# Mixer A's queries turned by VectorE, ScalarE and GpSimd instead of TensorE, the rotation on VectorE alone, and the score units one pair later

## The reference, cut to what matters

```
q_raw = q.reshape(b, N_KV_A, GROUP_A, s_len, dh) * scale
q_rot = rope(q, pos).reshape(b, N_KV_A, GROUP_A, s_len, dh) * scale
...
sc = jnp.einsum('bhgtd,bhcd->bhgtc', q_raw, kc)          # compressed branch: raw queries
p_cmp = jax.nn.softmax(jnp.where(c_valid, sc, NEG), axis=-1) * c_valid.any(-1)[:, None]
...
num, _, den = band_attention(q_rot, rope(k_win, pos), v_win, WIN - 1)   # window branch: rotated queries
o = gates[..., 0:1] * o_cmp + gates[..., 1:2] * o_slc + gates[..., 2:3] * o_win
```

## Time and profile before

| what | us |
|---|---|
| median of three runs (lowest to highest) | 1766.12 (1765.85 to 1766.53) |
| the profiled execution: its own time | 1765.85 |
| its span, first to last instruction | 1763.9 |
| TensorE busy (matmuls) | 1757.8 |
| VectorE busy | 1153.4 |
| ScalarE busy | 886.8 |
| GpSimd busy | 598.9 |

### The profile page before, as it was taken

The page is one execution under the profiler, slowest core; times in us unless marked ns, Lnnn a source line. Parts: engine busy times, 40 slices in busy tenths (PEclk is TensorE's granted clock), DMA queues, the critical chain, the costliest instruction groups (busy, mean ns, idle before and its releaser), DMA issues.

```text
span 1763.9 us, 22877 instructions
## 1 busy us (share of the span) xinstructions
PE 1757.8 (100%) x7902; PEld 1456.4 (83%) x7902; DVE 1153.4 (65%) x1192; ACT 886.8 (50%) x1216; POOL 598.9 (34%) x834
## 2 busy tenths in 40 slices
PE   9999999999999999999999999999999999999998
PEld 7888888888888888888888888888888888888886
DVE  7657656787888878656665666566655784444445
ACT  7643455464554545456435643564456554444443
POOL 3335303367593948721353034304431510000000
PEclk9999999999999999999999999999999999999999
DMA  9866687656565656666666666666666656667665
GB/s 294 254 199 188 188 248 229 179 161 185 157 189 151 185 160 174 183 197 182 179 195 196 182 181 197 194 190 176 191 194 191 190 185 217 213 213 212 213 202 204
DMA packets 184267, 344.77 MB, mean 195 GB/s; under 512 B 15216, under 2 KB 19568, under 8 KB 184176
## 3 DMA queue, kind: packets, MB, share of 16 engines
q1 hardware_dynamic: 183456, 342.58, 66.2%
q10 hardware_dynamic: 720, 0.93, 0.1%
HBM read 339.27 MB, written 4.19 MB: 195 GB/s over the span
## 4 chain that ended last, share of the span: by engine, by line
PE 99%; DMA 0%; ACT 0%; SPq 0%; DVE 0%; ACTq 0%; issue 0%
PE acc L640 31%; PE acc L646 31%; PE acc L643 31%; PE acc L821 1%; PE scores L810 0%; PE scores L709 0%; DMA raw<-in_w_in 0%; PE scores L742 0%; PE scores L741 0%; PE scores L740 0%; PE heads L757 0%; PE heads L758 0%; PE heads L759 0%; PE scores L665 0%; PE heads L692 0%; PE trans L657 0%
## 5 line engine op out<-in xcount | busy, mean ns | idle before, releaser
L1239 DVE TENSOR_TENSOR w_parts<-raw,w_parts 128x1024 fp32r<-128x1024 f32 x620 | 784.4, 1266 | 556.9 <-ACT w_parts L929 555.3
L929 ACT ACTIVATE w_parts<-raw 128x1024 fp32r<-128x1024 f32 x620 | 656.2, 1059 | 662.6 <-PE acc L646 649.6
L640 PE MATMUL acc<-w_parts,x_parts 128*128 128x512 f32 x2424 | 946.7, 391 | 0.2 <-DVE w_parts L1239 0.2
L646 PE MATMUL acc<-w_parts,x_parts 128*128 128x512 f32 x2424 | 943.8, 389 | 0.0
L643 PE MATMUL acc<-w_parts,x_parts 128*128 128x512 f32 x2424 | 943.3, 389 | 0.0
L646 PEld LDWEIGHTS acc<-w_parts,x_parts 128*128 128x128 f32 x2424 | 455.1, 188 | 95.8 <-DVE x_parts L1281 0.3
L640 PEld LDWEIGHTS acc<-w_parts,x_parts 128*128 128x128 f32 x2424 | 455.3, 188 | 93.4 <-issue 0.6
L643 PEld LDWEIGHTS acc<-w_parts,x_parts 128*128 128x128 f32 x2424 | 455.3, 188 | 93.0
L515 POOL COPY rot<-tok_b 32x256 f32<-32x256 f32 x120 | 86.9, 724 | 140.6 <-DVE tok_b L1613 135.7
L499 POOL TENSOR_TENSOR rot<-tok_a,trig 128x512 f32<-128x512 f32 x18 | 30.6, 1699 | 260.5 <-ACT tok_a L935 121.4
L515 POOL COPY b_first_t<-probs 32x128 f32<-32x128 f32 x64 | 31.1, 485 | 163.1 <-DVE probs L1686 160.6
(11 more groups left out here) (240 smaller groups left out, 1010.1 us busy)
## 6 DMA issues: line engine op xcount, KB each, us to landing
raw<-in_w_in SPq DMA_DIRECT2D x478, 512.0 KB, 3.7
raw<-in_w_out SPq DMA_DIRECT2D x128, 512.0 KB, 4.3
raw<-in_w SPq DMA_DIRECT2D x16, 512.0 KB, 4.7
x_tok<-in_x SPq DMA_DIRECT2D x16, 256.0 KB, 5.3
xt_raw<-in_x_t SPq DMA_DIRECT2D x7, 512.0 KB, 6.2
wpost<-in_post_w SPq DMA_DIRECT2D x8, 256.0 KB, 5.1
out<-y SPq DMA_DIRECT2D x3, 512.0 KB, 2.8
out<-y SPq DMA_DIRECT2D x5, 256.0 KB, 2.1
```

Source lines behind the costliest of these rows:

```text
L640: nc.tensor.matmul(o, stat_hi, mov_hi, start=(k == 0), stop=False)
L646: last = nc.tensor.matmul(o, stat_lo, mov_hi, start=False, stop=(k == KB - 1))
L929: nc.scalar.activation(w_hi[:, n % SPLIT_SLOTS, :, 0:width], raw[:, n % RAW_SLOTS, :, 0:width], ACT.Copy).then_inc(hi_ready, 1)
L1239: V.tensor_tensor(w_lo[:, s, :, 0:width], raw[:, n % RAW_SLOTS, :, 0:width], w_hi[:, s, :, 0:width].bitcast(F32), ALU.subtract).then_inc(l ...
```

## The change

TensorE's eight batches of four transposes go, and with them ScalarE's evacuations. VectorE transposes all of `tok_a` within its 32x32 blocks in one instruction at `at` 0; then GpSimd moves the eight blocks of the first 64 partitions and ScalarE the eight of the others (four at `at` 1, four at `at` 2) into `qraw_t`. GpSimd's part in the rotation goes: at `at` 2 VectorE multiplies both tiles by the cosines, makes the two crossed halves into `mixed`, and adds. The compressed scores move from pair 3 to pair 4, their product with the values from pair 11 to 12, the turn of their rows from `at` 5 to `at` 7. The units move from pairs 6, 7, 8, 10, 12, 14 to 7, 8, 9, 11, 13, 14. GpSimd's last two batches of moved probabilities are announced one after the other, not both at the end.

```diff
-UNIT_STEPS = {6: 0, 7: 1, 8: 2, 10: 3, 12: 4, 14: 5}
+UNIT_STEPS = {7: 0, 8: 1, 9: 2, 11: 3, 13: 4, 14: 5}
...
             def rotate_a(g):
-                for t in range(TILES):
...
-                    pool.wait_ge(tr_free, FILL_A + t + 1 + FILLS_A * g)
-                    nc.gpsimd.tensor_tensor(turned, qraw_t[:, :, cols], cos, ALU.mult).then_inc(q_cos_ready, 1)
-                    pool.wait_ge(q_cos_ready, t + 1 + 2 * g)
-                    pool.wait_ge(q_sin_ready, t + 1 + 2 * g)
-                    nc.gpsimd.tensor_tensor(turned, turned, crossed, ALU.add).then_inc(q_rot_ready, 1)
+                pool.wait_ge(q_turned, g + 1)
+                move_blocks(tok_a[:, :, :].rearrange("p t (h d) -> p t h d", h=HPG),
+                            qraw_t[:, :, :].rearrange("p h (t q) -> p t h q", t=TILES),
+                            range(QUARTERS * QUARTERS // 2)).then_inc(q_moved_pool, 1)
+                pool.wait_ge(q_moved_pool, g + 1)
                 pool.wait_ge(q_ready, 2 + 2 * g)
...
-                    last.then_inc(probs_moved, 1)
+                        if i == 1:
+                            last.then_inc(probs_moved, 1)
...
-                if n in (1, 2):
-                    t = n - 1
-                    pe.wait_ge(acc0_free if t == 0 else acc1_free, c)
-                    transpose4(tok_a[:, t, :], fill + t)
-                if n == 3:
-                    pe.wait_ge(tr_free, fill + 2)
+                if n == 4:
+                    pe.wait_ge(q_moved_pool, g + 1)
+                    pe.wait_ge(q_moved_act, g + 1)
...
-                if n == 11:
+                if n == 12:
                     pe.wait_ge(rows_moved, g + 1)
...
             def first_turned(u, g):
-                act.wait_ge(probs_moved, 3 * g + (1 if u < 2 else 3))
+                act.wait_ge(probs_moved, 3 * g + u // 2 + 1)
...
                     if at in (1, 2):
-                        take_fill(fill + at - 1, qraw_t[:, :, (at - 1) * P:at * P])
+                        if at == 1:
+                            act.wait_ge(q_turned, g + 1)
+                        for cols in range(QUARTERS):
+                            last = move_quarters(tok_a, qraw_t, at + 1, cols)
+                        if at == 2:
+                            last.then_inc(q_moved_act, 1)
...
+            def rotate_queries(g):
+                dve.wait_ge(q_moved_pool, g + 1)
+                dve.wait_ge(q_moved_act, g + 1)
...
+                V.tensor_tensor(turned, source, factor[1], ALU.mult)
                 for x in range(2):
...
+                    own, other = slice(x * 64, (x + 1) * 64), slice((1 - x) * 64, (2 - x) * 64)
+                    last = V.tensor_tensor(crossed[own, :, :, :], source[other, :, :, :], factor[0][other, :, :, :], ALU.mult)
                 last.then_inc(q_sin_ready, 1)
+                dve.wait_ge(q_sin_ready, g + 1)
+                V.tensor_tensor(turned, turned, crossed, ALU.add).then_inc(q_rot_ready, 1)
...
-                    if at in (2, 3):
-                        crossed_halves(at - 2, g, fill)
+                    if at == 0:
+                        dve.wait_ge(acc0_free, c)
+                        dve.wait_ge(acc1_free, c)
+                        V.transpose(tok_a[:, :, :], tok_a[:, :, :]).then_inc(q_turned, 1)
+                    if at == 2:
+                        rotate_queries(g)
...
+                    if at == 7:
+                        dve.wait_ge(probs_ready, unit + 1)
+                        rows = rows_c[:, :, :, :, :].rearrange("p t h a c -> p (t h a c)").bitcast(F32)
+                        V.transpose(rows, rows).then_inc(rows_turned, 1)
...
-                    if at == 5:
-                        dve.wait_ge(probs_ready, unit + 1)
-                        rows = rows_c[:, :, :, :, :].rearrange("p t h a c -> p (t h a c)").bitcast(F32)
-                        V.transpose(rows, rows).then_inc(rows_turned, 1)
```

More of the change, by code:

```diff
@@ L315, in build @@
         heads_taken = sem("heads_taken")
-        q_cos_ready = sem("q_cos_ready")
+        q_turned = sem("q_turned")
+        q_moved_pool = sem("q_moved_pool")
+        q_moved_act = sem("q_moved_act")
         q_sin_ready = sem("q_sin_ready")
@@ L651, in gemm_pair @@
                     last.then_inc(last_tile0, 1)
[L653 to L658, removed]
             def first_scores(unit, g):
@@ L727, in attention_a, with scores_a @@
                 if n in UNIT_STEPS:
-                    scores_a(UNIT_STEPS[n], g, unit, fill)
-            def scores_a(u, g, unit, fill):
+                    scores_a(UNIT_STEPS[n], g, unit)
+            def scores_a(u, g, unit):
                 t = UNIT_TILES_A[u]
@@ L864, in _, with attention_a_chunk @@
                 gemm_pair(C_QA0, n, 0)
-            def attention_a_chunk(c, g, fill, unit):
+            def attention_a_chunk(c, g, unit):
                 for n in range(PAIRS):
-                    attention_a(n, c, g, fill, unit)
+                    attention_a(n, g, unit)
                     gemm_pair(c, n, 1)
             for g in range(GROUPS - 1):
-                per = FILLS_A
-                attention_a_chunk(C_A + 2 * g, g, FILL_A + per * g, UNITS_A * g)
+                attention_a_chunk(C_A + 2 * g, g, UNITS_A * g)
                 for n in range(PAIRS):
@@ L876, in _ @@
                     gemm_pair(C_A + 1 + 2 * g, n, 0)
[L877 removed]
+            attention_a_chunk(C_B - 1, GROUPS - 1, UNIT_B - UNITS_A)
             for g in range(GROUPS):
@@ L1065, in move_quarters, with attention_a_frame @@
                                             ACT.Copy)
-            def attention_a_frame(c, g, fill, unit):
+            def attention_a_frame(c, g, unit):
                 for n in range(LEAD, PAIRS + LEAD):
@@ L1153, in _ @@
             with act.Fori(0, GROUPS - 1) as g:
-                per = FILLS_A
-                attention_a_frame(C_A + 2 * g, g, FILL_A + per * g, UNITS_A * g)
+                attention_a_frame(C_A + 2 * g, g, UNITS_A * g)
                 mixing_frame(C_A + 1 + 2 * g, 2 * g, g)
-            attention_a_frame(C_B - 1, GROUPS - 1, FILL_B - FILLS_A, UNIT_B - UNITS_A)
+            attention_a_frame(C_B - 1, GROUPS - 1, UNIT_B - UNITS_A)
             mixing_frame(C_B, 2 * (GROUPS - 1), GROUPS - 1)
@@ L1504, in rest_turned @@
                                 ).then_inc(pt_ready, 1)
[L1506 to L1510, removed]
+            def rotate_queries(g):
+                dve.wait_ge(q_moved_pool, g + 1)
+                dve.wait_ge(q_moved_act, g + 1)
+                by_tile = "p h (t q) -> p t h q"
+                turned = rot[:, :, :].rearrange("p t (h q) -> p t h q", h=HPG)
+                crossed = mixed[:, :, :].rearrange("p t (h q) -> p t h q", h=HPG)
+                factor = [turn_t[:, i, :].rearrange("p (t q) -> p t q", t=TILES).unsqueeze(2).broadcast_to([P, TILES, HPG, P])
+                          for i in range(2)]
+                source = qraw_t[:, :, :].rearrange(by_tile, t=TILES)
+                V.tensor_tensor(turned, source, factor[1], ALU.mult)
                 for x in range(2):
-                    dst, src = slice(x * 64, (x + 1) * 64), slice((1 - x) * 64, (2 - x) * 64)
-                    last = V.tensor_tensor(rot_tmp[dst, :].rearrange("p (h q) -> p h q", h=HPG), qraw_t[src, :, cols],
-                                           turn_t[src, 0, cols].unsqueeze(1).broadcast_to([64, HPG, P]), ALU.mult)
+                    own, other = slice(x * 64, (x + 1) * 64), slice((1 - x) * 64, (2 - x) * 64)
+                    last = V.tensor_tensor(crossed[own, :, :, :], source[other, :, :, :], factor[0][other, :, :, :], ALU.mult)
                 last.then_inc(q_sin_ready, 1)
+                dve.wait_ge(q_sin_ready, g + 1)
+                V.tensor_tensor(turned, turned, crossed, ALU.add).then_inc(q_rot_ready, 1)
             def turn_pair(u, unit):
```

21 lines of the change are left out of this document (6 added, 15 removed).

## The result

The changed kernel takes 1770.83 us, the median of 12 runs (1769.20 to 1772.90). The kernel before takes 1766.11 us beside it, the median of 12. The ratio is 1.0027, with a 95% interval of 1.0019 to 1.0034: slower by 0.27%. (One of the twelve runs of before took 2978.82 us and is left out of the ratio.) The forecast was 1767.0, its range ended at 1770.3, and the likeliest case was no measurable difference.

The account below looks back on a forecast made before the run. TensorE was taken as the bound: 3.8 us of transposes saved against 4.7 of new stall for VectorE's low part gives +0.9, so 1767.0 us on the median. The range was 1763.8 to 1770.3.

Parts of the forecast that it names:

- TensorE is the sum of what it is given: TensorE waits for nobody after the start, so the kernel's time is the sum of its work.
- the low part keeps up: Rival: VectorE's low part is ready in time and the whole 3.8 us is kept, 1762.3 us; chance 0.06.
- The transposes cost 0.47 per batch, and TensorE comes 0.95 earlier: On TensorE, eight batches of four cost 3.8 us; later points of each group are reached 0.95 us earlier.
- The place, the number and the order of the waits: TensorE waits for VectorE's low part at each group's first product with the values: 1.0, 1.5, 1.5 and 0.7 us.
- The start of the group: VectorE, from the first chunk's start in group two: rotation at 8.1 us, split of pair 6 at 14.9, before 14.3.
- The tail: VectorE and ScalarE from last mask to low part: 11.0 us, before 10.1; the added 0.9 is unit 4's scaling.
- The sum of the waits: New stall on TensorE over the four groups: together 4.7 us against 3.8 saved, so +0.9.
- a kinder one: Second ledger for group two's low part, ending 0.3 us earlier because the compressed softmax loses its contention; mean stall 1.5.
- A stall is lost for good: A stall on TensorE is lost, but behind it nothing more: VectorE catches up within the second chunk.
- the rivals: VectorE later by 0.7 us or more per group (0.16), low part in time (0.06), transposes costing their whole duration (0.01).
- The slower one: Rival: two more copies held by splits delay VectorE's rotation to 10.0, pair 5 missed by 0.5, 1774.6 us; chance 0.16.
- the two held copies of the forecast: Of GpSimd's eight copies at the group's start, one meets the split of pair 3, one that of pair 4.

Follow-up runs that it names:

- The first experiment: Changed kernel with the products with the values of units 0 and 1 moved from pairs 2 and 3 of the second chunk to 3 and 4: 1762.36 us.
- the last experiment: Changed kernel with the rotation's two half products reading their own 64 partitions instead of the other 64: 1769.06 us, ratio 1.0017.
- units 3 and 4 back: Changed kernel with its units at pairs 7, 8, 9, 10, 12, 14 instead of 7, 8, 9, 11, 13, 14: 1770.74 us, ratio 1.0027.
- the kernel with the long waits: Changed kernel with the first product with the values at pair 1 of the second chunk instead of 2: 1787.62 and 1787.63 us, ratio 1.0122.

## Why the prediction was wrong

Point by point, by its own steps.

- **TensorE is the sum of what it is given.** Right. The first experiment is that sum, with nobody waited for at the products: 1762.36, where the rival "the low part keeps up" had 1762.3.
- **The transposes cost 0.47 per batch, and TensorE comes 0.95 earlier.** Right: 0.48, and S+55.51 for 55.52.
- **The place, the number and the order of the waits.** Right: four, at the first product, for the low part, the fourth the shortest, none before pair 5.
- **The start of the group.** Right in its mechanism, 0.33 short in its sum. 0.2 of it is the start of the rotation (8.31 for 8.1). The rotation itself, from its first product to the split behind it, takes 4.87, where I had 4.7: three of its four instructions are followed after 1.24 or 1.25, not 1.15. The crossing of partitions is 0.09 of the first of these, shown by the last experiment. The next two hand over at 1.22 to 1.25 even without it, and the add is followed by the split after 1.14. One pattern fits all eight hand-overs of the two kernels: it is 1.22 to 1.25 where the next instruction begins to read or write on another half of the partitions than the one before it (the second half product writes the upper half after the lower, the add starts at the lower again), and 1.14 or 1.15 where both begin on the same. No run tries that by itself, and the add also waits for the half products' semaphore.
- **The tail.** The length was right (11.1 for 11.0), with some luck: the steps listed for it add up to 10.8. The reason given for the added 0.9 did not hold as a cost. I wrote that the scaling of unit 4 moved into the chain. Undoing just that shortened the tail to 10.08, but the wait of 1.93 us moved ahead of it and nothing was saved; putting all units back, so that none of 2 to 5 are adjacent, saved 0.6. VectorE and ScalarE have to do all of it between the split of pair 6 and the low part, and what seems to count is how long two units in a row leave VectorE with nothing to do. From the split of pair 6 to the low part it was 41.72 before and is 42.25 after: 0.53. So of a lateness of 1.47 (57.48 for 56.01), 0.94 comes from the start of the group and 0.53 from the units' places.
- **The sum of the waits.** 6.14 for 4.7. A part of it, 0.15 in each group, is the ledger averaged with a kinder one, for a gain that no row showed. The rest is the start of the group, and the first group, whose low part came at 56.69 where 56.4 was expected. With the ledger as it stood, 57.0 in the second group, the sum would have been about 5.3. (In the sum as recorded the first group's 1.0 is also 0.1 more than 1.5 less 0.6.)
- **"A stall is lost for good", and costs its own length.** This is the step that failed, in the prediction's words "behind the stall nothing more is lost". The rows of before show no stall of TensorE within the groups to check it on, and the cost behind one was put at nothing. After a stall TensorE was taken to go on as before. It doesn't: its first product costs 0.11 more, and after a wait of 2 us its clock can fall to its lower level for some eight matmuls, which costs 1.6 us. The forecast with the measured waits, 1762.36 + 6.14 + 0.45 = 1768.95, comes 0.25 to 0.5 under the lowest heap of the runs (1769.20 to 1769.45). One fall gives 1770.6 and the middle heap, two give 1772.2 and the upper one. So the three heaps fit with none, one and two falls. Only the profiled run shows where its clock fell; for the others the number is inferred from the time. Each run's mean granted clock goes the same way, as far as three digits can tell: 0.999 to 1.000 in the lowest heap, 0.998 or 0.999 in the middle one, 0.998 in the three runs of the upper one.

Between forecast and median lie 3.8 us. The waits are 1.4 of them, the first products 0.45, one fall of the clock 1.6; 0.3 remains. Without the clock the kernel would be at 1769.2, within the range and just inside "no measurable difference". The direction of the net sum (more lost in waits than gained in transposes) was right, its size was not.

None of the rivals was what happened. The slower one wanted two more copies held up by splits, and pair 5 missed. Only the two held copies of the forecast were seen, and within the groups TensorE waited for no split. The time came out on that rival's side for another reason.

**What stays open.** Why the clock falls after one wait of 2 us and not after another. In the profiled runs of three kernels with such waits (the changed one, units 3 and 4 back, without crossing) there are two each, of 1.95 to 2.02; in each of them the clock stayed after the one in group two and fell after the one in group three. In the profiled runs it never fell around those of 0.3 to 1.46, and always around those of 3.5 and more. I didn't try to move GpSimd's or ScalarE's copies so that the rotation starts sooner.

## What to carry to other kernels

When work is taken from the engine that sets the time, every hand-over to it comes earlier by what was saved up to that point: list the margins first, and move the consumers that have less. Here that one line in a table turned a loss of 4.7 us into a gain of 3.7. And price a new wait on TensorE at more than its length: in the profiled runs here the matmuls behind a wait of 2 us ran at half the clock in three cases of six, and filling such waits with work that nobody needs made the kernel faster.

## What the runs showed of the hardware that was not expected

- A TensorE that had worked without pause for nearly 100 us lost its full clock 1.3 us after a single wait of 2 us, and eight matmuls ran at half speed. The page's slices don't show it and the run's mean granted clock (0.999) hardly does; the lengths of single matmuls (0.63 for 0.39) and narrow windows do.
- The first matmul after a wait has a pitch of 0.34 instead of 0.23 at full clock, and of 0.59 in the kernel with the long waits, where the clock is low from the first product on in three groups of four.
- 3.6 us of matmuls that nobody reads, put into those waits, made the kernel 1.7 us faster.
- On VectorE, a half product that reads the other 64 partitions starts 1.24 us after the 128-partition product ahead of it, one that reads the first 64, which it also writes, 1.15. From half product to half product it is 1.22 to 1.24 either way.
